# Latent projections between the steps of differential attention, gate chunks between the units of latent attention

## Chip, cores and metric
The kernel runs on one core of a Trainium2 chip. The metric is the device time of one execution in microseconds, the median of several. In the text PE is TensorE, PEld its weight loads, DVE VectorE, ACT ScalarE, POOL GpSimd and SP SyncE.

## What is computed
Two transformer blocks on 512 tokens of width 1024, in float32. Cut to what matters here:

```python
xn = rmsnorm(x, norm_mix_g)
q_lat, kv_lat, k_rope, dq, dk, dv, gate_pre = split(xn @ w_in)      # 384, 256, 32, 512, 512, 512, 2048
q  = rmsnorm(q_lat, g_q) @ w_uq                                     # latent attention: 8 heads of 64 + 32
kv = rmsnorm(kv_lat, g_kv) @ w_ukv
o_mla = causal_attention(q with rope, k with shared rope key, v)
o1, o2 = causal_attention(rope(dq)[0 | 1], rope(dk)[0 | 1], dv)     # differential attention: 4 heads, 2 halves of 64
o_diff = rmsnorm(o1 - lam * o2, g_sub) * (1 - lambda_init)
gates = sigmoid(gate_pre + b_gate)
x = x + (g_mla * (o_mla @ w_a) + g_diff * (o_diff @ w_b)) @ w_out
x = x + swiglu(rmsnorm(x, g_ffn)); x = rmsnorm(x, g_final)          # ffn0
mod = silu(c) @ ada_w + ada_b                                       # 9 vectors of 1024, "ada"
# second block: swiglu (ffn1), a mixer of two attentions with gates, swiglu (ffn2),
# each with its norm scaled and shifted by mod
```

## The kernel before
**Products.** Activations lie as 128 features by 512 tokens. Each float32 operand is split into a high and a low part, so a product is three matmuls: high by high, high by low, low by high (`split_product`). Weights come as 311 chunks of 128x1024 in one fixed order (`STREAM`). SP loads a chunk into one of three `RAW` buffers, ACT makes its high half `HI` (`split_hi`), DVE its low half `LO` (`split_lo`), and TensorE uses it, 24 matmuls of 512 columns in most cases. ACT and DVE work two chunks ahead of TensorE. Each engine has its own program, written in a fixed order; semaphores tie them together. No scheduler moves anything.

**First block, stages in order.** `project_in1` makes the input projections: five latent tiles, the shared rope key and eight tiles of queries and keys, 14 chunks. Between them stand the norm of the input and the two latent norms, each a sum of squares by one-column matmuls (`norm_sums`), a root on ACT, a reciprocal on DVE and a spread by transposes (`norm_spread`). DVE takes each tile out of PSUM, scaled, and rotates it (`rope`). `token_major` makes the values, four chunks. `diff_attention` runs 16 pairs of units, a pair for four causal blocks (128 to 512 keys) of each of four heads. At step s TensorE makes the scores of pair s in four banks, the transposes of pair s-2 and the products with the values of pair s-3; DVE takes the maxima and combines the two halves, ACT makes the exponentials and copies the transposes.

Then come the expansions of the latents, five chunks with 102 matmuls, the latent attention `attention(1)`, 32 units in rounds of four, and `merge(0)`: for each of eight output tiles two gate chunks and a branch chunk. Its first part also turns both attention outputs (`turn`). `out_proj(0)`, a norm, and `ffn(0)` follow. The second block's attentions, `attention(2)` and `attention(3)`, already have gate chunks between their units, eight each, one for every round, taken out of bank 7 by ACT.

**ada.** 72 pieces of 128x1024 go through DVE, each multiplied by a column and added to `ACC`. After each eight TensorE sums them (`ada_sum`) and DVE adds the bias (`ada_take`). POOL loads them in two buffers. Eight pieces lie in `merge(0)`, eight in `out_proj(0)`, 56 in the gate and up projections of `ffn(0)`.

## Time and profile before

| | us |
|---|---|
| median of 3 runs | 2048.89 (2043.05 to 2051.16) |
| the profiled execution | 2047.24 |
| its span, first to last instruction | 2045.2 |
| PE busy | 2001.5 (98%) |
| DVE busy | 1030.8 (50%) |
| ACT busy | 708.8 (35%) |
| mean granted TensorE clock | 0.975 |

The span is what the instructions cover; the 2.0 us around it belong to the start and end of the execution. A matmul's recorded end is modelled, and matmuls overlap, so a busy PE isn't one at its peak: the granted clock stands beside it (1.00 is 2.4 GHz, 0.50 is 1.2 GHz). An engine's idle time is put down to what released it.

### The profile page before, as it was taken

The page shows a single profiled execution, that of the slowest core. Times are in us where ns is not written, and L with a number is a line of the kernel's source. Part 1 is how long each engine was busy: PE and PEld are TensorE (multiplying, and loading weights), DVE is VectorE, ACT ScalarE, POOL GpSimd, SP SyncE. Part 2 cuts the span into 40 slices and gives each one's busy share as a digit, 9 for nine tenths or more (in the row PEclk, how much of TensorE's full clock was granted, in tenths as well). Part 3 has the DMA queues.
Part 4 walks back from the last instruction along what each step waited for, and adds up shares of the span by engine and source line. Part 5 has one row for each costly group of instructions (what it writes and reads, how often), then busy time and mean ns, then how long its engine had stood idle before and what let it go on. Part 6 is the DMA issues. An engine that isn't in the chain of part 4 may idle for free. (4 is left out here: it accounts for less than half of the span.)

```text
span 2045.2 us, 25500 instructions
## 1 busy us (share of the span) xinstructions
PE 2001.5 (98%) x9134; PEld 1604.0 (78%) x9142; DVE 1030.8 (50%) x1587; ACT 708.8 (35%) x1196; POOL 78.0 (4%) x113
## 2 busy tenths in 40 slices
PE   8989999999999999999999999999999999999999
PEld 6765778887888888788888877767777878888887
DVE  6664555567656533453334335857833654333322
ACT  5223662234222222332222324435544533223221
POOL 0010000001111100000000010400000000000000
PEclk9885999999999999999999999999999999999999
DMA  5210113455776633233233332221111223232332
GB/s 191 62 62 0 52 32 115 133 164 177 222 220 204 205 102 103 77 105 101 92 99 96 104 102 83 63 62 42 42 42 42 83 82 103 92 103 92 103 103 92
DMA packets 57514, 207.11 MB, mean 101 GB/s; under 512 B 6448, under 2 KB 6576, under 8 KB 57440
## 3 DMA queue, kind: packets, MB, share of 16 engines
q1 hardware_dynamic: 46800, 167.68, 25.9%
q0 software_dynamic: 10640, 38.44, 6.1%
q8 instruction: 47, 0.77, 0.2%
q14 instruction: 27, 0.22, 0.0%
HBM read 203.96 MB, written 2.10 MB: 101 GB/s over the span
## 5 line engine op out<-in xcount | busy, mean ns | idle before, releaser
L1340 DVE TENSOR_TENSOR LO<-RAW,HI 128x1024 fp32r<-128x1024 f32 x311 | 381.8, 1228 | 512.7 <-ACT HI L955 511.1
L389 PE MATMUL PS<-XH,HI 128*128 128x512 f32 x1552 | 625.2, 403 | 8.0 <-DVE LO L1340 4.9
L391 PE MATMUL PS<-XH,LO 128*128 128x512 f32 x1552 | 608.3, 392 | 0.0
L390 PE MATMUL PS<-XL,HI 128*128 128x512 f32 x1552 | 607.6, 392 | 0.0
L955 ACT ACTIVATE HI<-RAW 128x1024 fp32r<-128x1024 f32 x311 | 327.9, 1056 | 586.1 <-PE PS L391 568.3
L389 PEld LDWEIGHTS PS<-XH,HI 128*128 128x128 f32 x1552 | 294.2, 190 | 82.5 <-issue 13.9
L391 PEld LDWEIGHTS PS<-XH,LO 128*128 128x128 f32 x1552 | 293.2, 189 | 62.9
L390 PEld LDWEIGHTS PS<-XL,HI 128*128 128x128 f32 x1552 | 294.2, 190 | 55.0
L389 PE MATMUL PS<-HIDH,HI 128*128 128x512 f32 x528 | 205.4, 389 | 0.0
L390 PE MATMUL PS<-HIDL,HI 128*128 128x512 f32 x528 | 205.4, 389 | 0.0
L391 PE MATMUL PS<-HIDH,LO 128*128 128x512 f32 x528 | 205.4, 389 | 0.0
L390 PEld LDWEIGHTS PS<-HIDL,HI 128*128 128x128 f32 x528 | 99.1, 188 | 20.7
L389 PEld LDWEIGHTS PS<-HIDH,HI 128*128 128x128 f32 x528 | 99.1, 188 | 20.6
L391 PEld LDWEIGHTS PS<-HIDH,LO 128*128 128x128 f32 x528 | 99.1, 188 | 20.4
L1237 ACT ACTIVATE T<-PS 128x512 f32<-128x512 f32 x45 | 26.9, 598 | 164.0 <-PE PS L391 163.8
L1490 DVE SCALAR_TENSOR_TENSOR ACC<-ADA,SM,ACC 128x1024 f32<-128x1024 f32 x57 | 73.0, 1281 | 13.1 <-DMA ADA<-ada 12.9
L1894 DVE TENSOR_TENSOR Y<-T,PS 128x512 f32<-128x512 f32 x45 | 30.9, 688 | 94.2 <-PE PS L391 94.2
L1165 ACT ACTIVATE PT<-PS 128x128 f32<-128x128 f32 (+1 forms) x96 | 42.1, 439 | 84.5 <-PE PS L736 84.4
L1737 DVE TENSOR_REDUCE SM<-PS 128x1 f32<-128x128 f32 (+1 forms) x96 | 47.0, 489 | 32.9 <-PE PS L723 12.9
L1175 ACT ACTIVATE P<-PS,SM 128x128 f32<-128x128 f32 (+1 forms) x96 | 50.5, 526 | 26.7 <-DVE SM L1737 25.6
L326 POOL DMA_DIRECT2D ADA<-ada x70 | 36.9, 528 | 547.5 <-DVE ACC L1488 271.4
L1243 ACT ACTIVATE HIDH<-Y 128x512 f32 (+1 forms) x66 | 41.7, 631 | 25.8 <-DVE Y L1894 25.8
(328 smaller groups left out, 2131.4 us busy)
## 6 DMA issues: line engine op xcount, KB each, us to landing
RAW<-weights SPq DMA_DIRECT2D x311, 512.0 KB, 3.5
ADA<-ada POOLq DMA_DIRECT2D x72, 512.0 KB, 4.6
X<-x_in SPq DMA_DIRECT2D x4, 512.0 KB, 7.0
y_out<-X SPq DMA_DIRECT2D x8, 256.0 KB, 4.6
SQC<-squares SPq DMA_DIRECT2D x1, 320.0 KB, 9.3
T<-positions POOLq DMA_DIRECT2D x1, 256.0 KB, 5.2
POS<-positions POOLq DMA_DIRECT2D x1, 256.0 KB, 3.3
LAMS<-lambdas POOLq DMA_DIRECT2D x1, 128.0 KB, 6.2
```

The source lines that it names most:

```text
L326: pool.dma_start(ADA[j][:], ada[2 * i + (j + 2)]).then_inc(sem(f"ada{j}"), 16)
L389: mm(bank, a, moving[0][:, t, :], start=start, stop=False)
L390: mm(bank, a, moving[1][:, t, :], start=False, stop=False)
L391: ins = mm(bank, z, moving[0][:, t, :], start=False, stop=stop)
L955: A(HI[n0 % 3][:], RAW[n0 % 3][:], ACT.Copy).then_inc(sem("hi_ready"), 1)
L1165: A(at_["PT"][v % 2][:, 0:n], PS[:, 3 + v % 2, 0:n], ACT.Copy).then_inc(sem("pt_copied"), 1)
L1175: A(at_["P"][u % 3][:, 0:n], PS[:, u % 3, 0:n], ACT.Exp, bias=NMX[:, u % 4:u % 4 + 1], accum_out=RSU[:, u % 4:u % 4 + 1]).then_inc(sem("pr ...
L1243: A(HIDH[:, bass.ds(t, 1), :], Y[:, 0:1, :], ACT.Copy).then_inc(sem("hid_hi"), 1)
L1340: V.tensor_tensor(LO[n0 % 3][:], RAW[n0 % 3][:], HI[n0 % 3][:].bitcast(F32), ALU.subtract)\
L1490: V.scalar_tensor_tensor(out=ACC[:], in0=ADA[j][:], scalar=CND[:, kt:kt + 1], in1=ACC[:], op0=ALU.mult, op1=ALU.add).then_inc(sem("ada_add ...
L1737: V.tensor_reduce(NMX[:, u % 4:u % 4 + 1], PS[:, u % 3, 0:n], AX, ALU.max, negate=True)\
L1894: V.tensor_tensor(Y[:, 0, :], SILU[j % 3], PS[:, 2 * (j % 3) + 1, :], ALU.mult)\
```

## The change
The stream's order is new. Eight chunks of queries and keys come first, in pairs of one head, then two value chunks. The differential attention starts when its first head is rotated; the two other value chunks follow its first two scores. From step 2 on, 22 pieces of latent work (`latent_work`) stand between its matmuls, one or two a step (`piece_step`): the six latent input chunks in halves, their norms, and the expansions. They use banks 5 and 6 in turn and bank 7 for the norms, so the scores have three banks, the transposes one and the products one. ACT now takes query, key and latent tiles out unscaled; the input norm's factor is multiplied into the rotary table and the latent roots.

The 16 gate chunks of the first block stand between the units of `attention(1)`, one for two units, in bank 7, taken out by DVE into tiles of their own. After it come the turns, as after `attention(3)`, and `branch(0)`, the same code as the second block's, with the sigmoids. `merge` is gone.

The ada pieces move: 56 stay in the gate and up projections, now the first seven groups, and eight each lie in the first two and the last two output tiles of `ffn(0)`. Its eighth sum stands in the output projection, its ninth in the norm after it, in the place of a matmul that only kept TensorE busy. POOL loads the first two pieces when the latent scores are done. The weights are the same, in another order; no product is added or left out.

```diff
-STREAM = (("in1", 14), ("dv1", 4), ("uq", 3), ("uk", 1), ("uv", 1), ("merge1", 24), ("out1", 8),
+STREAM = (("qk1", 8), ("dv1", 4), ("lat1", 6), ("uq", 3), ("uk", 1), ("uv", 1), ("gates1", 2 * DT),
+  ("branch1", 8), ("out1", 8),
...
+LATENT = ("q0", "q1", "q2", "k0", "k1", "kr", "uq0", "uq1", "uq2", "uq3", "uq4", "uq5", "uk0", "uk1", "uk2",
+          "uk3", "uv0", "uv1", "uv2", "uv3")
...
+def piece_step(p):
+    return 2 + p if p < 5 else 7 + (p - 5) // 2 if p < 15 else p - 3
+LATENT_CHUNKS = {piece_step(2 * c): c for c in range(11)}
...
-    for j in range(2):
-        pool.dma_start(ADA[j][:], ada[j]).then_inc(sem(f"ada{j}"), 16)
...
+    pool.wait_ge(sem("scores"), 2 * NU)
+    for j in range(2):
+        pool.dma_start(ADA[j][:], ada[j]).then_inc(sem(f"ada{j}"), 16)
...
+    def project_qk1():
+        n0 = FIRST["qk1"]
+        behind(0, n0, (0, 1))
+        pe.wait_ge(sem("squares_loaded"), 16)
+        norm_sums(0)
+        for j in range(2, 8):
+            w = chunk(n0 + j, 0, 0)
+            if j >= 4:
+                pe.wait_ge(sem("qk_copied"), j - 3)
+            used(split_product(PS[:, j % 4, :], w, range(8), range(8), (XH, XL)))
             if j == 2:
                 norm_spread(0)
-        released["in_copied"] += len(IN1)
...
+        def sums(k):
+            nt = NORMS[k][0]
+            pe.wait_ge(sem("squared"), NTB[k + 1])
+            if k == 2:
+                pe.wait_ge(sem("normed"), NDB[2])
+            for t in range(nt):
+                for b in range(NB):
+                    ins = mm(S_LAT[:, b:b + 1], LSQ[k][:, t, b * P:(b + 1) * P], SQV["ones"][:, 0:1],
+                             start=t == 0 and b == 0, stop=t == nt - 1 and b == NB - 1)
+            ins.then_inc(sem("sq_summed"), 1)
+        def spread(k):
+            pe.wait_ge(sem("expanded"), k + 1)
+            for b in range(NB):
+                tok = slice(b * P, (b + 1) * P)
+                ins = nc.tensor.transpose(PS[:, 7, tok], RB[:, 1, tok], SQV["ident"])
+            ins.then_inc(sem("rstd"), 1)
+        pe.wait_ge(sem("v_copied"), NB)
+        for k, t in enumerate(("q0", "q1", "q2", "k0", "k1", "kr")):
+            to = bank_for(t)
+            w = chunk(FIRST["lat1"] + k, 0, 0)
+            split_product(to, w, range(4), range(4), (XH, XL), last=False)
+            if t == "k0":
+                sums(1)
+            if t == "k1":
+                spread(1)
+            yield
+            used(split_product(to, w, range(4, 8), range(4, 8), (XH, XL), first=False))
+            yield
+        for j in range(3):
+            w = chunk(FIRST["uq"] + j, 0, 0)
...
+                ins = split_product(to, w, range(3 * r, 3 * r + 3), range(3), (LQH, LQL))
+                if r:
+                    used(ins)
+                else:
+                    ins.then_inc(sem("uq_half"), 1)
+                if r == 0 and j < 2:
+                    (sums, spread)[j](2)
+                yield
+        w = chunk(FIRST["uk"], 0, 0)
...
+        latent = latent_work()
         for s in range(NPAIR + 3):
+            pieces = [p for p in range(22) if piece_step(p) == s]
             if s < NPAIR:
                 p, i = divmod(s, NB)
                 n = P * (i + 1)
-                if s >= 2:
...
+                    pe.wait_ge(sem("qk_rotated"), 2 * p + 2)
                 for r in range(2):
-                    bank = PS[:, SCORE_BANKS[s % 2][r], :]
+                    if 2 * s + r >= 3:
+                        pe.wait_ge(sem("probs"), 2 * s + r - 2)
+                    bank = PS[:, (2 * s + r) % 3, :]
                     mm(bank[:, 0:n], q_diff(2 * p + r, i), k_diff(2 * p + r, n), start=True, stop=False)
                     mm(bank[:, n - P:n], IDENT_B[:], CAUSAL_B[:], start=False, stop=True)\
                         .then_inc(sem("scores"), 1)
+            if s < 2:
+                diff_values(2 + s)
+            if pieces:
+                next(latent)
             if 2 <= s < NPAIR + 2:
                 w = s - 2
+                pe.wait_ge(sem("combined"), w + 1)
                 if w == 0:
                     pe.wait_ge(sem("v_copied"), NB)
-                pe.wait_ge(sem("combined"), w + 1)
-                if w >= 2:
-                    pe.wait_ge(sem("pt_copied"), w - 1)
+                else:
+                    pe.wait_ge(sem("pt_copied"), w)
                 for kb in range(w % NB + 1):
-                    ins = nc.tensor.transpose(PS[:, 3 + w % 2, kb * P:(kb + 1) * P],
+                    ins = nc.tensor.transpose(PS[:, 3, kb * P:(kb + 1) * P],
                                               P1[w % 3][:, kb * P:(kb + 1) * P], SQV["ident"])
                 ins.then_inc(sem("pt"), 1)
+            if len(pieces) == 2:
...
-                if w >= 2:
-                    pe.wait_ge(sem("onorm"), w - 1)
+                if w:
+                    pe.wait_ge(sem("onorm"), w)
                 for kb in range(i + 1):
-                    ins = mm(PS[:, 5 + w % 2, 0:P], PT1[w % 2][:, kb * P:(kb + 1) * P],
+                    ins = mm(PS[:, 4, 0:P], PT0[w % 2][:, kb * P:(kb + 1) * P],
                              DV[:, kb, p * P:(p + 1) * P], start=kb == 0, stop=kb == i)
                 ins.then_inc(sem("pv"), 1)
     def attention(a):
         at_ = ATT[a]
-        n0 = FIRST["gates2"] + DT * (a - 2)
+        n0, per, before = GATE_CHUNKS[a]
...
                 return
-            if u % 4 == 0:
+            if per == 2:
+                blocks = (((), (0, 1, 2)), ((3, 4), (5, 6, 7)))[u % 2][part]
+            elif u % 4 == 0:
...
+                if before + c:
+                    pe.wait_ge(sem("gate_copied"), before + c)
+            ins = split_product(PS[:, 7, :], (n0 + c) % 3, blocks, blocks, (XH, XL),
+                                first=blocks[0] == 0, last=blocks[-1] == 7)
+            if blocks[-1] == 7:
                 used(ins)
         for u in range(NU + 3):
...
                 if a == 1 and u == 2:
                     pe.wait_ge(sem("v_copied"), 2 * NB)
+                    pe.wait_ge(sem("onorm"), AFTER[1])
...
+    def after_attention(a):
+        turn(a - 1, (3,))
+        for f in range(4):
+            pe.wait_ge(sem("onorm"), AFTER[a] + 2 * NB * (f + 1))
+            turn(a, (f,))
...
-            latents(j)
+            if 1 <= j <= 8:
+                act.wait_ge(sem("chunk_used"), n0 + j)
+                dst, scale = QK1[j - 1]
+                A(dst, PS[:, (j - 1) % 4, :], ACT.Copy, scale=scale).then_inc(sem("qk_copied"), 1)
+            if j == 1:
+                table(0, TAB_A1)
+            if j == 9:
+                act.wait_ge(sem("lams_used"), 2)
+                A(LAM[:, 2:4], LAM[:, 0:2], ACT.Exp).then_inc(sem("lam_exp"), 1)
...
+    def latent_copies(p):
+        def done(t):
+            return sem(LATENT_FREE[t][0])
+        if p < 10 and p % 2:
+            k = p // 2
+            act.wait_ge(sem("chunk_used"), FIRST["lat1"] + k + 1)
+            n, t = (1, k) if k < 3 else (2, k - 3)
...
+            if pieces:
+                latent_copies(pieces[0])
+            if s == 2:
+                table(1, TAB_P1)
+            if s in (8, 11):
+                stds(1 if s == 8 else 2)
+            if s in (9, 12):
+                k = 1 if s == 9 else 2
+                for t in range(NORMS[k][0]):
+                    high(k, t)
...
+    def rotate_qk(k):
+        dst = QK1[k][0]
+        v.wait_ge(sem("qk_copied"), k + 1)
+        rope(dst, TAB_A1, "rot_a")
+        V.tensor_tensor(dst, T[:, 0, :], T[:, 1, :], ALU.add).then_inc(sem("qk_rotated"), 1)
+        v.wait_ge(sem("qk_rotated"), k + 1)
...
+                v.wait_ge(sem("pos_loaded"), 16)
+                link(V.tensor_copy(pos, pos.bitcast(I32)))
+                angles(0, pos, "freq_a")
+            if j == 2:
                 lambdas()
...
+                v.wait_ge(sem("table"), 1)
+                for c in range(2):
+                    link(V.tensor_tensor(TAB_A1[:, c, :], TAB_A1[:, c, :], R0[:], ALU.mult))
+            if j >= 3:
+                rotate_qk(j - 3)
...
+            if s == 0:
+                rotate_qk(7)
+            if s == 1:
+                angles(1, TAB_P1[:, 0, :], "freq_p")
+            if s in (8, 11):
+                roots_of(1 if s == 8 else 2)
+            if s in (9, 12):
+                latent_norm(1 if s == 9 else 2)
+            if s == 10:
+                shared_keys()
+            if s == 13:
+                rotate_shared_keys()
+            if s in (14, 15):
+                rotate_queries(s - 14)
...
+            if a == 1 and u % 2 == 0 and 2 <= u <= NU:
+                c = u // 2 - 1
+                v.wait_ge(sem("chunk_used"), n0 + c + 1)
+                V.tensor_tensor(gate_tile(a, c), PS[:, 7, :], R0[:], ALU.mult).then_inc(sem("gate_copied"), 1)
...
-                    ada_piece(16 + 3 * j, 8, i)
+                    ada_piece(0 + 3 * j, 8, i)
...
-                    ada_piece(17 + 3 * j, 8, i)
+                    ada_piece(1 + 3 * j, 8, i)
...
-                    ada_piece(18 + 3 * j, 8, i)
+                    ada_piece(2 + 3 * j, 8, i)
...
                 for g in range(3):
                     split_lo(n0 + 3 * j + g, 6, i)
+                    if f == 0 and isinstance(i, int) and g < 2:
+                        for r in range(2):
+                            ada_piece((64 if i else 56) + 4 * j + 2 * g + r)
                 v.wait_ge(sem("chunk_used"), 6 * i + (n0 + 3 * j + 3))
```

**Order, first place: TensorE in a step of the differential attention.** One step before, with 128 keys. DK and DQ are keys and queries (one tile DQK after), SQC the identity, P the probabilities, PT the copied transposes.

```order
L657 MATMUL PS<-DK,DQ 128x128 [waits probs]
L658 MATMUL PS<-CAUSAL_B,IDENT_B 128x128
L657 MATMUL PS<-DK,DQ 128x128
...
L669 MATMUL PS<-SQC,P_0_86 128x128 [waits pt_copied,combined]
L669 MATMUL PS<-SQC,P_0_86 128x128 x2
L679 MATMUL PS<-DV,PT_1_90 128x128 [waits onorm,pt_copied]
```

The step of the same head's first block after (step 8). LO and HI are weights, XH and XL the input; RB holds a latent norm's reciprocals.

```order
L767 MATMUL PS<-DQK 128x128 [waits probs,qk_rotated]
L768 MATMUL PS<-CAUSAL_B,IDENT_B 128x128
L767 MATMUL PS<-DQK 128x128 [waits probs]
...
L422 MATMUL PS<-XH,HI_55 128x512
...
L783 MATMUL PS<-SQC,P_0_85 128x128 [waits pt_copied,combined]
...
L422 MATMUL PS<-XH,HI_56 128x512 [waits lo_ready,even_free]
...
L694 MATMUL PS<-SQC,RB 128x128 [waits expanded]
...
L795 MATMUL PS<-DV,PT_1_91 128x128 [waits onorm,pt_copied]
```

Twelve matmuls stand ahead of the transposes and twelve behind them, and the transposes of RB, the latent norm's spread, stand ahead of the products with the values.

**Second place: ACT at the start.** Before, three chunks' high halves are made ahead of the first rotary table (TAB_A).

```order
L988 ACTIVATE SM_74<-PS,SM 128x4 [waits sq_summed]
L955 ACTIVATE HI_55<-RAW_52 128x1024 [waits chunk_used,raw0]
L955 ACTIVATE HI_56<-RAW_53 128x1024 [waits chunk_used,raw1]
L955 ACTIVATE HI_57<-RAW_54 128x1024 [waits chunk_used,raw2]
L1014 ACT_TABLE_LOAD
L1014 ACTIVATE TAB_A_84<-Y 128x512 [waits angle]
L1015 ACTIVATE Y<-Y 128x512
L1017 ACTIVATE TAB_A_84<-Y,SM 128x512 [waits absolute]
L969 ACTIVATE SQ<-LATQ 128x512 [waits sq_summed,in_copied] x2
```

After:

```order
L1055 ACTIVATE SM_74<-PS,SM 128x4 [waits sq_summed]
L1019 ACTIVATE HI_55<-RAW_52 128x1024 [waits chunk_used,raw0]
L1095 ACTIVATE DQK<-PS 128x512 [waits chunk_used]
L1081 ACT_TABLE_LOAD
L1081 ACTIVATE TAB_A_83<-Y 128x512 [waits angle]
L1082 ACTIVATE Y<-Y 128x512
L1084 ACTIVATE TAB_A_83<-Y,SM 128x512 [waits absolute]
L1019 ACTIVATE HI_56<-RAW_53 128x1024 [waits chunk_used,raw1]
```

The table stands ahead of the second of them, for chunk 4, and waits for DVE's angles (Y).

**Third place: DVE in the latent attention.** Two units before (OM is the output).

```order
L1737 TENSOR_REDUCE SM<-PS 128x1 [waits probs,scores]
L1756 RECIPROCAL SM<-SM 128x1 [waits probs]
L1760 TENSOR_SCALAR OM<-PS,SM 128x64 [waits pv,dve_link]
L1737 TENSOR_REDUCE SM<-PS 128x1 [waits probs,scores]
L1756 RECIPROCAL SM<-SM 128x1 [waits probs]
L1760 TENSOR_SCALAR OM<-PS,SM 128x64 [waits pv,dve_link]
```

After:

```order
L1881 RECIPROCAL SM<-SM 128x1 [waits probs]
L1885 TENSOR_SCALAR OM<-PS,SM 128x64 [waits pv,dve_link]
L1855 TENSOR_REDUCE SM<-PS 128x1 [waits probs,scores]
L1881 RECIPROCAL SM<-SM 128x1 [waits probs]
L1885 TENSOR_SCALAR OM<-PS,SM 128x64 [waits pv,dve_link]
L1847 TENSOR_TENSOR GATE_1D<-PS,R_75 128x512 [waits chunk_used]
L1855 TENSOR_REDUCE SM<-PS 128x1 [waits probs,scores]
L1419 TENSOR_TENSOR LO_58<-RAW_52,HI_55 128x1024 [waits hi_ready]
```

A gate's scaled copy (GATE_1D) and a split (LO) came in for every two units; the copy stands behind the output scaling that waits for `pv`.

## Rows read from the trace of the kernel before
**Rows 1.** The page: TensorE's granted clock in 40 slices; a chunk's two splits.
```profile
PEclk9885999999999999999999999999999999999999
...
L1340 DVE TENSOR_TENSOR LO<-RAW,HI 128x1024 fp32r<-128x1024 f32 x311 | 381.8, 1228 | 512.7 <-ACT HI L955 511.1
...
L955 ACT ACTIVATE HI<-RAW 128x1024 fp32r<-128x1024 f32 x311 | 327.9, 1056 | 586.1 <-PE PS L391 568.3
```
**Rows 2.** Busy time by stage: us, PE, PEld, DVE, ACT, POOL, clock, DMA.
```profile
12.24:139.13 126.89, 114.32 (x493) 93.14 (x493) 84.70 (x133) 39.93 (x53) 9.12 (x12) 0.93 0.31 98
139.13:209.31 70.18, 68.38 (x218) 39.43 (x217) 34.02 (x95) 26.77 (x85) 0.00 (x0) 0.59 0.01 2
143.50:197.00 53.50, 53.50 (x151) 29.98 (x151) 24.95 (x70) 17.09 (x59) 0.00 (x0) 0.50 0.00 0
209.31:235.09 25.78, 23.41 (x105) 19.07 (x104) 14.84 (x23) 16.27 (x26) 0.00 (x0) 1.00 0.26 82
235.09:284.05 48.96, 48.65 (x336) 38.31 (x337) 27.01 (x96) 36.59 (x130) 0.00 (x0) 0.97 0.04 12
284.05:423.20 139.15, 136.10 (x610) 113.15 (x610) 76.81 (x102) 45.42 (x58) 3.69 (x7) 0.99 0.38 114
1480.60:1576.90 96.30, 96.28 (x485) 69.87 (x492) 33.07 (x94) 39.90 (x108) 0.00 (x0) 1.00 0.14 44
```
**Rows 3.** Timeline of TensorE, differential attention: start, us, line, operation.
```profile
164.44 2.07 PE L657 MATMUL PS<-DK,DQ 64*128 64x512 f32 x2
...
183.51 2.07 PE L657 MATMUL PS<-DK,DQ 64*128 64x512 f32 x2
...
201.79 1.12 PE L657 MATMUL PS<-DK,DQ 64*128 64x512 f32 x2
```
**Rows 4.** TensorE's waits, whole run: us in total, times, longest.
```profile
PE PS L389 <- DVE LO L1340: 4.9, 2, 3.3
PE PS L490 <- DVE DK L1526: 4.6, 1, 4.6
PE PS L463 <- DVE Y L1429: 3.5, 1, 3.5
...
PE PS L718 <- DVE QM L1996: 2.4, 1, 2.4
...
PE PS L389 <- ACT GATE_F L1149: 2.2, 7, 0.7
```
**Rows 5.** Timeline of TensorE at three other places.
```profile
67.24 1.05 PE L440 MATMUL PS<-SQC,RB 128*128 128x1 f32 x8 [1.18 <-DVE RB L1375]
...
118.17 0.63 PE L491 MATMUL PS<-LO,XH 128*128 128x512 f32 x1
...
261.73 1.08 PE L718 MATMUL PS<-KM,QM 96*128 96x512 f32 x2
...
267.56 1.08 PE L718 MATMUL PS<-KM,QM 96*128 96x512 f32 x2
```
**Rows 6.** Timeline of DVE, then of ACT, at the first table of angles.
```profile
36.57 0.43 DVE L1469 TENSOR_SCALAR Y<-Y 128x512 f32<-128x512 f32 x1
36.91 1.22 DVE L1340 TENSOR_TENSOR LO<-RAW,HI 128x1024 fp32r<-128x1024 f32 x1
...
37.03 0.63 ACT L1014 ACTIVATE TAB_A<-Y 128x512 f32<-128x512 f32 x1 [3.88 <-DVE Y L1469]
...
38.21 0.72 ACT L1017 ACTIVATE TAB_A<-Y,SM 128x512 f32<-128x512 f32 x1
```
**Rows 7.** Groups of DVE, then ACT, 20 to 283 us: busy, mean ns.
```profile
L1996 DVE TENSOR_TENSOR QM<-T 32x512 f32<-32x512 f32 x8 | 5.5, 684 | 0.2
...
L1138 ACT ACTIVATION_READ_ACCUMULATOR P<-PS,SM 128x1 f32 x16 | 3.3, 206 | 0.0
...
L1138 ACT ACTIVATE P<-PS,SM 128x512 f32<-128x512 f32 x4 | 2.7, 683 | 0.0
L988 ACT ACT_TABLE_LOAD x2 | 2.6, 1283 | 0.0
```

764 lines of the change are left out of this document (345 added, 419 removed).

## The prediction
> **What bounds the kernel now.** Read three views in this order. First the page: TensorE is busy nearly everywhere, so only two things can give time back, waits of TensorE and stretches of lower clock. The clock row shows the latter: 8, 8 and 5 in the second to fourth of its 40 slices, 9 nearly everywhere else [rows 1]. Then the stages [rows 2]. The differential attention (139.13 to 209.31) takes 70.2 us at a mean clock of 0.59; its middle, 143.5 to 197, is busy without a gap for all 53.5 us at 0.50, while its DVE is busy for 24.95 us and its ACT for 17.09. No engine feeds it too slowly: it is TensorE at 1.2 GHz that sets the time. The timeline shows the price [rows 3]: a score of 512 keys takes 2.07 us at 183.51 and 1.12 at 201.79, once 2.4 GHz is granted again, and a round of four steps takes 183.51 - 164.44 = 19.07 us. Third the waits of TensorE [rows 4]: the projections before this stage lose 4.9 (one of it 3.3 at the start), 4.6 and 3.5 us to DVE, and the stage after it 2.4. All other stages are filled: the latent attention holds 48.65 busy us of 48.96, the merge 136.10 of 139.15 [rows 2].
>
> **The early part, up to the first score of the latent attention.** Before, it runs from 12.24 to 235.09 us, 222.9 us. No matrix work is dropped, so I add up what TensorE has to do at full clock. A chunk of 24 matmuls costs 5.46 us: the merge has 24 of them in 139.15 us less some 8 for its turns. So one matmul of 512 columns costs 0.2275 us.
> - Eight chunks for queries and keys and four for values: 12 x 5.46 = 65.5 us.
> - The differential attention at full clock: four rounds of 19.07 / 2 = 38.1 us.
> - The latent work moved between its steps: six input chunks (144 matmuls) and 102 for the expansions, 246 x 0.2275 = 56.0 us.
> - The norms' sums, 28 blocks at 1.05 / 4 us [rows 5], are 7.4, their three spreads some 1 us.
> - Each change between the two kinds of work costs a little. Attention (3) of the kernel before is built this way: 96.3 us for eight rounds with a gate chunk each [rows 2]. A bare round is 267.56 - 261.73 = 5.83 us [rows 5], so 96.3 - 8 x (5.83 + 5.46) = 6.0 us, over 56 pieces at most 0.11 each; 22 pieces cost 2.4.
>
> That is 170.4 us. It holds only at 2.4 GHz. For that speaks the same attention (3): scores of 64 rows, as here, turns and values of the same kind, with dense matmuls between, and its clock is 1.00 [rows 2]. Now the new waits; five edits put something into a queue ahead of something else.
> - At the start ACT now makes the rotary table ahead of the high half of chunk 4 (the second order piece). Before, DVE's angles ended at 37.0 and the low half followed at once, to 38.13 [rows 6]; TensorE had waited for it for 4.9 - 3.3 = 1.6 us [rows 4]. Now sine, absolute and sine come first, 37.03 to 38.93, then 1.05 for the high half and 1.23 for the low [rows 1, 6]: the low half ends at 41.3, and TensorE waits some 4.8 us. The lambdas and two scalings of the table (3 us) then stand ahead of the next split; it still ends by 45.5, while chunk 4 lasts to 46.7, and from there a rotation and a split (4.2) fit into a chunk.
> - At steps 8 and 11 TensorE reaches a norm's spread one piece (2.7 and 2.0 us) after the transpose. In that time ACT must copy the transpose, make two exponentials (at 512 keys 0.68 + 0.21 us each [rows 7]), copy and square or copy twice a latent tile (1.2 to 1.3), load a table (1.28 [rows 7]) and take the root, and DVE must expand it (1, with the handovers 1.5). That is about 6.0 and 6.5 us, so waits of 3.3 and 4.4. The nearest rows are the 3.5 and 4.6 us that the same norms cost before [rows 4]; from below the bound is 0.
> - The second table, at step 2, puts two table loads and 2 us of ACT ahead of the exponentials of step 3: 1.6 us.
> - Steps 12 to 15 give DVE 4 x 2.2 us of its own (24.95 us of 53.5, by a step of 19.07 / 4 [rows 2, 3]), two splits (2.5), the second latent norm (2.9), one rotation (2.9) and two query rotations of seven operations (4.8 each [rows 7]): 26.7 us. TensorE has 22 us until it needs the result, a wait of 5. From below 0, from above 12 if ACT and DVE wait for one another.
> - Where TensorE has waited the clock falls: after the 4.6 us wait the matmuls at 118.17 still take 0.63 us instead of 0.40 [rows 5], a stretch of some 3.3 us that costs half of itself. Three such dips are 5 us.
>
> Together 170.4 + 4.8 + 7.7 + 1.6 + 5 + 5 = 194.5 us, a gain of 28.4. The 2.4 us wait for the rotated queries goes: DVE has them at step 15. The shared keys on POOL are copied behind step 13, some 25 us before their use.
>
> One rule weighs against this gain. TensorE is busy for all of 143.5 to 197 and stays at 0.50 [rows 2]. The Trainium skill, "TensorE: Matmul & The Clock Gate", section "Part 1: The HAM clock gate", says that idleness throttles the array and that sustained work releases it. By that rule the stage should have come back by itself, and its low clock would belong to no kind of work that one could mend by mixing; the trace disagrees, being busy is not enough here. The third rival is the time that it would give.
>
> **Latent attention with gate chunks, then the branches.** Before, 48.96 + 139.15 = 188.1 us [rows 2]. The gates leave the merge and stand between the units, two chunks a round. TensorE was full in both stages, so this saves no matrix time: 8 x 5.83 = 46.6, 16 x 5.46 = 87.4, 48 pieces at 0.11 = 5.3, 32 turns 4.2, eight branch chunks 43.7. The one bank for gates adds a wait: a new chunk starts when DVE has scaled the last one out, and that copy stands behind the output scaling that itself waits for TensorE (the third order piece). The nearest row is the wait for the same copy on ACT: 2.2 us in 7 waits, the longest 0.7 [rows 4]. I take 0.5 for each of 16, 8 us; between 0 and 11. Sum 195.2, a loss of 7.1 us. It eats the 3 us that the merge spent waiting for its turned outputs and the 2 to 3 us of low clock at the start of the stage.
>
> **ada pieces.** All 72 multiplications and 9 sums stay. The 16 of merge and output projection, each a pass over 128x1024 like a split's 1.23 us [rows 1], were under TensorE's work; now they lie in the first two and last two output tiles of ffn0, some 5 us of DVE a tile beside 66 matmuls, 15 us. POOL starts the loads when the latent scores end, over 50 us before ffn0. If the cover failed, each late split would cost up to 1.3 us. The last sum fills an idle place in the norm; the last modulation, some 1 us on DVE, comes ahead of ffn1's next split. Nothing in all, within 1.5 us either way.
>
> **Sum.** 28.4 - 7.1 = 21.3 us less. The profiled execution took 2047.24 us, 2.0 over its span; by the sum the new one takes 2025.9. The median of the runs, 2048.89, lies 1.65 above the profiled one, and I keep that distance: 2027.6, rounded to 2028 us.
>
> **Rivals.**
> - **The waits are hidden.** ACT and DVE catch up, TensorE never waits at spreads, tail or gates: 7.7 + 5 + 8 + 3.3 (two dips) = 24 us more, 2004 us. For it: both are half idle in these stages. Against: the waits of the same norms before.
> - **DVE becomes the bound.** It has some 79 us to do from step 0 on (35.7 its own, 13.5 for 11 splits, 7.3 norms, 15.4 rotations, 4.1 angles, 3 the rest) in about 130, in a fixed order. If each new wait in the list is twice as long, 7.7 + 1.6 + 5 + 8 = 22 us are lost, 2050 us.
> - **The low clock belongs to no work.** A stretch as long as 143.5 to 197 runs at half clock whatever fills it, so half of its 53.5 us, 26.7, is lost again: 2055 us. For it: nothing in DVE or ACT marks the point where the clock fell. Against: no other dense stage shows it. It is what the rule of the Trainium skill above comes to.
> - **The mixture stays at 1.2 GHz.** This ends slower. From step 2 to 18 TensorE has some 100 us of work at full clock. At 0.50 it takes 200, and the 21 us of waits and dips vanish under it: 79 us lost, 2107 us. It is slower than before from the point where over 21 of those 100 us run at half clock. For it: the transposes and scores that fell to 0.50 are all still there, and steps 2 to 6 and 12 to 15 hold only one piece each. Against: attention (3) at 1.00, with as little between its steps.
>
> **Chances.** Forecast 0.65, own range 2016 to 2040; hidden waits 0.12; DVE 0.11; clock of no work 0.04; half clock 0.08. Out of the 80% range I leave the half clock and the ends: 2004 to 2052. A measurement of this kernel tells some 0.5%, 10 us, from no change. Below 2038.6 lie nearly all of the forecast and the hidden waits, 0.76; within 10 us the DVE and clock rivals and the forecast's edge, 0.15; above, 0.09.
>
> **What would show it.** In the profile of after: clock near 1 from the first differential score to the last; first score of the latent attention at 206 to 208 us; a wait of over 4 us for the low half of chunk 4; two waits at the latent spreads; some 0.5 us for each gate copy; output projection starting at 402. A clock of 0.5 in the fused stage, or DVE busy over nine tenths there, would prove me wrong.

## The result and the profile after

| | before | after |
|---|---|---|
| median, 8 runs each in the same comparison | 2049.32 (2043.05 to 2060.35) | 2061.62 (2052.72 to 2066.81) |
| ratio to before | | 1.0068, 95% interval 1.0036 to 1.0100 |
| the profiled execution, its span | 2047.24, 2045.2 | 2064.44, 2062.4 |
| mean granted TensorE clock | 0.975 | 0.98 |

The change makes the kernel 0.7% slower. The forecast was 2028 us, 21 less than before, so it is wrong in sign and by 34 us in size. A second measurement of the same kernel (after_again below) gave 1.0077 (1.0049 to 1.0106).

First the page of after: its clock row, and the group of the ada pieces on DVE.

```profile
PEclk8988999999999999999999999999999999999999
...
L1576 DVE SCALAR_TENSOR_TENSOR ACC<-ADA,SM,ACC 128x1024 f32<-128x1024 f32 x63 | 80.8, 1282 | 31.4 <-DMA ADA<-ada 31.1
```

The 5 of [rows 1] is gone, yet 8s stand in the third and fourth slice, and in the first, where before had a 9. Then the stages of after as windows (us, busy time and instructions of PE, PEld, DVE, ACT and POOL, granted clock, DMA share, GB/s): from the first matmul to the first differential score, on to the first latent score, on to the output projection, on to the first down matmul of ffn0, on to the first score of `attention(2)`.

```profile
12.35:80.98 68.63, 62.90 (x261) 50.91 (x261) 46.22 (x77) 26.46 (x37) 1.27 (x2) 0.91 0.34 103
80.98:240.41 159.43, 134.24 (x559) 96.95 (x559) 76.55 (x162) 69.50 (x146) 5.61 (x8) 0.87 0.15 44
240.41:433.19 192.78, 186.13 (x947) 149.70 (x946) 90.47 (x190) 82.59 (x187) 1.06 (x2) 1.00 0.22 69
433.19:739.02 305.83, 304.60 (x1389) 250.78 (x1388) 179.44 (x195) 89.92 (x115) 29.68 (x56) 0.99 0.59 186
739.02:1399.16 660.14, 646.85 (x2906) 522.84 (x2904) 317.15 (x410) 210.98 (x286) 39.19 (x41) 0.99 0.32 101
```

Two windows of before to set beside them, the same early part and the stage from the first down matmul on:

```profile
12.24:235.09 222.85, 206.11 (x810) 151.63 (x811) 133.55 (x251) 82.97 (x164) 9.12 (x12) 0.83 0.21 66
729.47:1382.62 653.15, 643.19 (x2876) 519.15 (x2874) 298.48 (x392) 210.97 (x286) 31.72 (x27) 0.99 0.29 91
```

| stage | before | after | forecast |
|---|---|---|---|
| to the first latent score | 222.9 | 228.1 | 194.5 |
| latent attention to output projection | 188.1 | 192.8 | 195.2 |
| output projection to first down matmul | 306.3 | 305.8 | as before |
| first down matmul to `attention(2)` | 653.2 | 660.1 | as before |
| the rest | 662.6 | 663.2 | as before |

So the miss lies in two stages: 33.6 us in the early part, 7 in the one that got the ada pieces. Neither of the prediction's own signs of being wrong appears: the clock of the fused stage (the differential attention with the latent work between its steps, the second window) is 0.87 and not 0.5, and its DVE is busy for 76.55 of 159.43 us, under half. But the first latent score comes at 240.4 us instead of 206 to 208.

**The early part, taken apart.** Busy time times clock is what TensorE had to do at 2.4 GHz, busy time less that is what the low clock cost, and the rest of the window is waiting. For after: 62.90 x 0.91 + 134.24 x 0.87 = 174.0 us of work; 197.1 - 174.0 = 23.1 lost to the clock; 228.1 - 197.1 = 30.9 of waits. The clock has two digits, so each part is good to some 2.5 us.

| early part | length | work | waits | low clock |
|---|---|---|---|---|
| before | 222.9 | 171.1 | 16.7 | 35.0 |
| forecast | 194.5 | 170.4 | 19.1 | 5.0 |
| after | 228.1 | 174.0 | 30.9 | 23.1 |

The work was forecast within 4 us. Against the forecast the waits are 12 us longer, and the low clock costs 18 more. Where TensorE waits, from 12 to 241 us (total, times, longest; the first wait for LO, 4.5 us, ends at the first matmul and is outside the table above):

```profile
PE PS L694 <- DVE RB L1482: 9.8, 2, 5.9
PE PS L422 <- DVE LO L1419: 8.5, 2, 4.5
PE PS L422 <- ACT KM L1204: 3.8, 1, 3.8
PE PS L767 <- ACT P L1244: 2.9, 2, 1.8
PE PS L795 <- DVE OD L1793: 2.2, 3, 1.7
PE PS L686 <- ACT LSQ L1179: 2.1, 1, 2.1
PE PS L526 <- issue: 1.7, 1, 1.7
PE PS L422 <- ACT DV L1227: 1.5, 1, 1.5
```

The timeline of TensorE shows what stands behind such waits: a score at step 4, the first latent sums, both latent spreads, the third piece of the key expansion.

```profile
109.54 0.49 PE L767 MATMUL PS<-DQK 64*128 64x128 f32 x2 [1.76 <-ACT P L1244]
...
136.98 4.54 PE L686 MATMUL PS<-SQC,LSQ 128*128 128x1 f32 x24 [2.12 <-ACT LSQ L1179]
...
155.81 1.11 PE L694 MATMUL PS<-SQC,RB 128*128 128x128 f32 x4 [3.94 <-DVE RB L1482]
...
192.96 1.11 PE L694 MATMUL PS<-SQC,RB 128*128 128x128 f32 x4 [5.89 <-DVE RB L1482]
...
224.39 0.80 PE L422 MATMUL PS<-LKH,HI 128*128 128x512 f32 x1 [3.82 <-ACT KM L1204]
```

The 24 one-column matmuls at 136.98 take 0.19 us each, where eight took 1.05 us before, 0.13 each [rows 5], and the 512-column matmuls run at 0.63 us until 147.8; those behind the first spread until 164.7. Seven such stretches lie in the early part: 12.4 to 18.4, 43.5 to 49, 110.5 to 114, 137 to 147.8, 155.8 to 164.7, 193 to 199.3 and 224.4 to 230. Each starts at a wait of TensorE or within 1 us behind it, the first one at the wait for the first weights. The forecast had three, of 3.3 us each. Not every wait has one: nothing follows the 1.74 us at 69.9 or the 1.51 at 98.4.

### The profile page after: what moved, and what is told of

It is laid out like the page before. It is cut to its first block and busy times, and to the rows that moved or that the text cites. A ratio compares the mean times of both kernels' runs of the same rounds, so it can differ in the third digit from the quotient of the medians.

```text
span 2062.4 us, 25412 instructions
## 1 busy us (share of the span) xinstructions
PE 1996.8 (97%) x9148; PEld 1599.4 (78%) x9148; DVE 1016.0 (49%) x1576; ACT 721.8 (35%) x1215; POOL 77.0 (4%) x113
## 5 line engine op out<-in xcount | busy, mean ns | idle before, releaser
L422 PE MATMUL PS<-XH,HI 128*128 128x512 f32 x1552 | 632.9, 408 | 18.7 <-DVE LO L1419 8.5
L1576 DVE SCALAR_TENSOR_TENSOR ACC<-ADA,SM,ACC 128x1024 f32<-128x1024 f32 x63 | 80.8, 1282 | 31.4 <-DMA ADA<-ada 31.1
```

Of the source, the lines that this page charges most:

```text
L422: mm(bank, a, moving[0][:, t, :], start=start, stop=False)
L1576: V.scalar_tensor_tensor(out=ACC[:], in0=ADA[j][:], scalar=CND[:, kt:kt + 1], in1=ACC[:], op0=ALU.mult, op1=ALU.add).then_inc(sem("ada_add ...
```

## Experiments

The theory after this reading: the mixture does bring the full clock, as forecast, but its queues are too tight, and most waits of some length are paid twice, once itself and once by a stretch at half clock behind it. The main rival: the low clock belongs to the mixture's own short matmuls and would be there without the waits.

Medians are of 9 or 10 runs where nothing else is said. The runs of before beside them had a median of 2046.5 (beside the later spreads, first table and ada sum, and six idle matmuls), 2045.2 (query rotations, splits, second table, stall probe), 2044.4 (one and two idle matmuls, fixed_four, fixed_seven) and 2044.6 (the last three). A ratio given here differs from the quotient of the two medians by up to 0.002.

The single edits are small against the scatter of the runs (some 4 us), so each is read by its stage in the trace too: "early part" is the time from the first matmul to the first latent score, 228.1 us in after. How much a stage scatters by itself can be read where an edit lies elsewhere: the fused stage took 159.4, 159.2, 159.3 and 159.4 us in after, after_again, sum_later and ada_back, so 2 us tell something there; the first stage, the same code in eight traces, took 65 to 69 us, because the stretches at half clock at its start and behind the wait at 43.5 differ in length.

### Later spreads
```diff
-                    if t == "k1":
-                        spread(1)
                     yield
                     used(split_product(to, w, range(4, 8), ...))
+                    if t == "k1":
+                        spread(1)
                     yield
...
-                        if r == 0 and j < 2:
+                        if (j, r) in ((0, 0), (1, 1)):
                             (sums, spread)[j](2)
```


> The changed kernel with both latent spreads (transposes of RB) one piece later: the first behind the second half of the last latent key chunk in step 9, the second behind the second half of the second query chunk in step 12. Nothing else differs. The changed kernel's trace has waits of 3.9 and 5.9 us there, each followed by TensorE at half clock (155.8 to 164.7 and 193 to 198.5). Theory 'each wait brings its own dip': both waits go and the two dips with them, 9.8 + 4.4 + 2.7 = 17 us less, 2061.6 to 2045. Rival 'the low clock there comes from the mixture (one-column sums, transposes, 64-row scores)': only the waits go, 10 us, 2052, and the stretch behind the first spread stays at 0.50. Rival 'DVE and ACT are late anyway': the wait reappears at the first expansion of the queries, under 5 us gained, 2057 or more.

Measured: 2047.90 us, ratio to before 1.0004 (0.9980 to 1.0029). Windows up to the first differential and the first latent score:

```profile
12.29:79.42 67.13, 61.40 (x260) 49.73 (x260) 46.23 (x77) 26.47 (x37) 1.27 (x2) 0.92 0.35 106
79.42:224.90 145.48, 128.55 (x559) 93.58 (x559) 76.24 (x162) 69.59 (x146) 5.61 (x8) 0.92 0.16 48
```

The fused stage is 13.9 us shorter (159.4 to 145.5). By the same arithmetic the early part holds 174.8 us of work, 22.7 of waits and 15.2 of low clock: 8.2 of waits and 7.9 of clock went, the matmuls being the same. (The two waits of 9.8 us are gone; 0.9 and 1.1 us came up elsewhere.) The rival said that only the waits would go, and that the stretch behind the first spread would stay; it is gone. What the edit did not touch stayed: the wait of 2.1 us ahead of the sums and its half clock.

### Later first table
```diff
-                    if j == 1:
+                    if j == 2:
                         table(0, TAB_A1)
```


> The changed kernel with the first rotary table on ACT behind the high half of chunk 4 instead of ahead of it. Theory 'that place alone makes the wait at 39 us': the wait for the low half falls from 4.0 us to some 0.5, and the half clock behind it (43.5 to 48.8) goes: 3.5 + 2.6 = 6 us less, 2055.5. Rival 'the wait only moves': the rotations of queries and keys start 1 to 2 us later and TensorE waits the same at the first scores of step 0 or at the next split, under 2 us gained, 2060.

Measured: 2057.32 us, 1.0070 (1.0040 to 1.0100). The first matmul of chunk 4:

```profile
39.23 0.50 PE L422 MATMUL PS<-XH,HI 128*128 128x512 f32 x1 [0.99 <-DVE LO L1419]
```

The wait falls from 4.0 us to 1.0 and its half clock is gone. The first stage takes 61.8 us instead of 68.6, of which some 1 to 1.5 is the start; the fused stage then takes 2.1 us more, with a half clock at 91.5 that after doesn't have. Net 4 to 5 us in the trace, about as much as the first stage scatters by itself; the median alone could not show it. What is sure is the wait: it is 4.0 us in every trace with the table in its first place.

### Later query rotations
```diff
-                    if s in (14, 15):
-                        rotate_queries(s - 14)
+                    if s in (15, 16):
+                        rotate_queries(s - 15)
```


> The changed kernel with the two query rotations on DVE (seven operations each, 5.8 and 4.9 us in its trace) one step later, behind steps 15 and 16 instead of 14 and 15. Theory 'they stand ahead of the maxima of step 15, behind which the key copies on ACT are late': the wait of 3.8 us for a key copy (KM) with its half clock (223.5 to 230.5) and the 1.7 us for the output scaling go, 3.8 + 3 + 1.7 = 8.5 us less, 2053. Rival 'DVE is full there': the output scalings of steps 16 and 17 wait for the rotations instead, and the products with the values behind them, 3 us gained or less, 2059.

Measured: 2053.81 us, 1.0062 (1.0038 to 1.0086). The piece that waited 3.82 us at half clock:

```profile
217.25 0.50 PE L422 MATMUL PS<-LKH,HI 128*128 128x512 f32 x1 [2.67 <-ACT KM L1204]
```

The fused stage takes 153.6 us instead of 159.4, 5.8 less. The 1.7 us for the output scaling went, but of the 3.8 only 1.1: the four key copies on ACT (0.6 us each) are a limit by themselves. The half clock behind that wait is gone all the same. That was partly luck: the same wait of 2.67 us, in the same place, is followed by half clock in splits_behind (221.6) and in fixed_seven (188.6).

### Splits behind the exponentials
```diff
 # ACT; DVE likewise, behind the combination of its step
-                    if s in LATENT_CHUNKS:
-                        split_hi(FIRST["lat1"] + LATENT_CHUNKS[s])
...
                     if pieces:
                         latent_copies(pieces[0])
+                    if s in LATENT_CHUNKS:
+                        split_hi(FIRST["lat1"] + LATENT_CHUNKS[s])
```
In after the chain to the first spread reads so on ACT, in the timeline:

```profile
148.88 1.06 ACT L1019 ACTIVATE HI<-RAW 128x1024 fp32r<-128x1024 f32 x1 [11.47 <-PE PS L424]
...
151.50 0.37 ACT L1244 ACTIVATE P<-PS,SM 128x128 f32<-128x128 f32 x1 [1.18 <-DVE SM L1809]
...
153.30 1.28 ACT L1055 ACT_TABLE_LOAD   x1
```

And beside it on DVE:

```profile
149.97 1.23 DVE L1419 TENSOR_TENSOR LO<-RAW,HI 128x1024 fp32r<-128x1024 f32 x1 [7.36 <-ACT HI L1019]
151.12 0.48 DVE L1809 TENSOR_REDUCE SM<-PS 128x1 f32<-128x128 f32 x2
```

> The changed kernel with the latent chunks' splits (HI on ACT, LO on DVE) behind the exponentials, latent copies and the combination of their step instead of ahead of the maxima. They are needed two steps later. Theory 'the waits at sums and spreads are longer than forecast because a split of 1.1 and 1.2 us, itself released only by TensorE's last matmul on that buffer, stands ahead of the maxima': TensorE's wait ahead of the first latent sums (2.1 us) goes to 0.5 or less, the spreads' 3.9 and 5.9 shrink by about 2.3 each, and where a wait falls under some 2 us its half clock goes too: 6.5 us of waits and 4 of clock, 10 less, 2051. Rival 'the chain hangs on TensorE's own transposes and exponentials': the waits shrink by under 1 us in all, 2060.

Measured: 2060.65 us, 1.0072 (1.0044 to 1.0100). TensorE's waits:

```profile
PE PS L694 <- DVE RB L1482: 7.2, 2, 4.3
PE PS L795 <- DVE OD L1793: 6.5, 2, 4.0
```

The wait for the squares (2.1) is gone and the spreads' waits fall from 9.8 to 7.2, so the split does stand in that chain. But waits of 2.5 and 4.0 us for the output scaling come up instead of 1.7, with their half clock, and the fused stage takes 161.6 us. The attribution holds, the remedy doesn't: the split is only late for someone else.

This run also says something on the main rival. The latent sums no longer wait, and TensorE has had no wait since 107 us:

```profile
132.15 2.73 PE L686 MATMUL PS<-SQC,LSQ 128*128 128x1 f32 x24
...
137.83 0.63 PE L422 MATMUL PS<-XH,HI 128*128 128x512 f32 x1
```

The sums themselves run at full clock, 0.11 us each, but a few short matmuls later, from about 136.1 to 139.2, the clock is at half. So of the 10.8 us that follow the sums in after, some 3 come without any wait, with the one-column and short matmuls alone; the other 8 or so aren't there in this run, in which the wait is gone. Here the rival is right in part.

### Later second table
```diff
-                    if s == 1:
+                    if s == 5:
                         angles(1, TAB_P1[:, 0, :], "freq_p")
...
-                    if s == 2:
+                    if s == 7:
                         table(1, TAB_P1)
```


> The changed kernel with the second rotary table's angles on DVE at step 5 instead of 1 and the table on ACT at step 7 instead of 2. Theory 'two table loads and three passes on ACT hold the exponentials of step 3': the wait of 1.8 us for a probability at 109.5 and the half clock behind it (110.5 to 114.5, 1.7 us) go: 3.5 us less, 2058, if step 7 with two pieces of matrix work hides the same 4.5 us of ACT. Rival 'the table costs the same wherever it stands': the wait and a longer half clock appear at the transposes of step 8 or the first spread, no gain or up to 4 us lost, 2062 to 2066.

Measured: 2057.62 us, 1.0061 (1.0039 to 1.0084). Step 4's first score and the first spread:

```profile
108.62 0.48 PE L767 MATMUL PS<-DQK 64*128 64x128 f32 x2 [0.34 <-ACT P L1244]
...
154.64 1.11 PE L694 MATMUL PS<-SQC,RB 128*128 128x128 f32 x4 [5.21 <-DVE RB L1482]
```

Theory and rival both came true in part: 1.8 us fell to 0.3 with no half clock behind it, and 3.9 grew to 5.2. The fused stage took 157.0 us, 2.4 less.

### A later sum of the ada pieces
```diff
                 two(0)
                 if f == 0:
+                    two(1)
                     ada_sum(7)
-                with pe.Fori(1, 4) as i:
+                with pe.Fori(2 if f == 0 else 1, 4) as i:
```
The wait in after:

```profile
772.01 2.97 PE L650 MATMUL PS<-SQC,ACC 128*128 128x1 f32 x16 [2.91 <-DVE ACC L1576]
```

> The changed kernel with the eighth sum of the ada pieces on TensorE two output tiles later in the down projection of ffn0 (behind the fourth tile instead of the second). The pieces, their loads and DVE's order are the same. Theory 'the loads of the pieces are too slow for the sum's place': the wait of 2.9 us and the half clock behind it (772 to 779.3) go, some 6.5 us less, 2055, and the stage from the first down matmul to the second block's attention returns from 660.2 to some 654. Rival 'the loads contend with the weight loads or DVE is late with its splits': the stage stays at 660 and the time at 2061.

Measured: 2060.06 us, 1.0080 (1.0051 to 1.0108). The wait is gone and the stage took 654.6 us in this trace, but the time didn't move. The stage was 659.9, 658.5, 661.6, 655.5 and 653.6 in the five kernels above, which all have the sum in its old place, so one trace of it proves little. The two combined kernels below also have the later sum, and there the stage took 656.5 and 660.1 us: the later sum is no sure gain. The undo below had to decide.

### What a wait costs: the stall probe
In the kernel before, out_proj on TensorE and ACT:
```diff
+                    if m in (3, 5, 7):
+                        pe.wait_ge(sem("stall"), 3 * b + m // 2)
...
+                    if m in (3, 5, 7):
+                        for q in range(((1, 5, 10), (3, 8, 15))[b][m // 2 - 1]):
+                            A(SM[:, 85:86], EPSC, ACT.Copy)  # each waits for the last
...
```


> The kernel before, in which TensorE has to wait six times in dense matmul work (ahead of the fourth, sixth and eighth chunk of both output projections, some 11 us apart) for a chain of 2, 6, 11 and 4, 9, 16 small copies on ACT. It measures what a wait costs besides itself. Theory 'the clock falls by the length of the wait': waits under some 2 us leave the matmuls behind them at full speed, longer ones put a stretch of 3 to 6 us behind them at half clock (0.63 instead of 0.40 us each), so that a wait of 4 us costs 6 or more. Rival 'the half clock in the changed kernel's fused stage comes from its one-column and short matmuls': no wait here is followed by more than 3.3 us at half clock, whatever its length.

One run, 2066.22 us. The six waits (the edit makes each of them wait for the chain on ACT; what stands in the brackets is inferred by the profile):

```profile
431.46 0.47 PE L389 MATMUL PS<-MH,HI 128*128 128x512 f32 x1 [1.62 <-ACT SM L1230]
...
445.14 0.47 PE L389 MATMUL PS<-MH,HI 128*128 128x512 f32 x1 [2.52 <-DVE LO L1352]
...
461.59 0.76 PE L389 MATMUL PS<-MH,HI 128*128 128x512 f32 x1 [3.69 <-issue]
...
1651.31 0.47 PE L389 MATMUL PS<-MH,HI 128*128 128x512 f32 x1 [2.09 <-ACT SM L1230]
...
1665.69 0.77 PE L389 MATMUL PS<-MH,HI 128*128 128x512 f32 x1 [3.22 <-DVE LO L1352]
...
1684.50 0.77 PE L389 MATMUL PS<-MH,HI 128*128 128x512 f32 x1 [4.86 <-issue]
```

| wait, us | 1.62 | 2.09 | 2.52 | 3.22 | 3.69 | 4.86 |
|---|---|---|---|---|---|---|
| matmuls at 0.63 us behind it, us | 0 | 0 | 3.3 | 6.0 | 5.2 | 4.3 |
| cost: the wait and half of that stretch | 1.6 | 2.1 | 4.2 | 6.2 | 6.3 | 7.0 |

With nothing but dense 512-column matmuls around them, the four waits of 2.5 us and more were each followed by half clock, for up to 6.0 us, and the two of 1.6 and 2.1 by none. That refutes the rival as expected of this run, that no stretch would be longer than 3.3 us; it doesn't say that short matmuls bring no half clock of their own. Two things don't fit a simple price: the stretch isn't longer for a longer wait, and in the mixture 1.76 us was enough once while 2.12 and 3.94 us were followed by 10.8 and 8.9. The Trainium skill, "TensorE: Matmul & The Clock Gate", section "HAM oscillation — how this bites in real kernels", has an example in which each wait for data brings some 1.67 us of throttled time; here none of these stretches is as short as that.

This run brought a surprise. Its differential attention is the code of before, yet it took 56.2 us instead of 70.2. Two windows in it:

```profile
145.00:166.00 21.00, 21.00 (x61) 11.37 (x59) 10.39 (x29) 7.53 (x27) 0.00 (x0) 0.52 0.00 0
166.00:193.00 27.00, 25.36 (x126) 14.57 (x126) 19.50 (x57) 13.61 (x47) 0.00 (x0) 0.99 0.00 1
```

The same kind of work ran at 0.52 and then at 0.99. In the profile of before it stayed at 0.50 to 197 [rows 2]. And the runs of before, 29 in the first comparison, spread over 20 us in step with their clock: 2033.6 at a mean of 0.982, 2053.7 at 0.972. So the length of that stretch differs from run to run with nothing changed, 21 us in one trace and over 53.5 in the other; that it also makes the spread of the times is argued from the clock, two traces don't show it.

### Idle matmuls in the kernel before
```diff
                             pe.wait_ge(sem("probs"), 2 * s - 2)
+                        for t in range(6):   # 2 in filler_two, 1 in filler_one
+                            mm(PS[:, SCORE_BANKS[s % 2][0], :], XH[:, t, 0:P], XH[:, t, :], ...)
                         for r in range(2):
```


> The kernel before with six more matmuls of 512 columns (the input's high part by itself) ahead of the scores of each of the 16 steps of the differential attention, written into the score bank and overwritten: 96 matmuls, 21.8 us at full clock, that compute nothing. Theory 'this stage runs at half clock for want of dense matmuls between its own': the clock goes to near 1.00 and the stage takes 38.1 + 21.8 = 60 to 64 us instead of 70.2, so the kernel with more work is 6 to 10 us faster than before, 2041. Rival 'the low clock belongs to no kind of work': the stage stays at 0.50 and takes 70.2 + 43.7 = 114 us, 2093.

> The kernel before with two idle matmuls of 512 columns ahead of the scores of each step of the differential attention instead of six (filler_before): 32 in all, 7.3 us at full clock. With six the stage took 65.5 us at clock 1.00, so 65.5 - 21.8 = 43.7 us without them. Theory 'a few dense matmuls a step hold the clock': 43.7 + 7.3 = 51 us instead of 70.2 in the profiled execution, the time 18 us under before, 2028, with a smaller scatter. Rival 'two are not enough': stretches at 0.50 remain, the stage takes 60 us or more, and the runs scatter over some 20 us like those of before (2034 to 2054 here).

> The same with one idle matmul a step, 3.6 us. If the clock holds: 43.7 + 3.6 = 47.3 us for the stage, 22 under before, 2024. If it holds in part only: 55 to 65 us and a wide scatter, 2032 to 2042. In the stall probe, whose code in this stage is that of before, the stage began at 0.50 and returned to 1.00 at 166 with nothing else in it, so the outcome here also tells whether that return was chance.

The differential attention with six idle matmuls a step:

```profile
141.98:207.46 65.48, 63.55 (x307) 39.77 (x307) 33.52 (x95) 25.82 (x84) 0.00 (x0) 1.00 0.00 1
```

With two:

```profile
140.45:192.76 52.31, 50.87 (x247) 29.86 (x247) 33.10 (x95) 26.63 (x85) 0.00 (x0) 0.97 0.00 1
```

With one:

```profile
140.68:190.12 49.44, 48.08 (x233) 28.53 (x232) 33.03 (x95) 26.71 (x85) 0.00 (x0) 0.97 0.00 1
```

| | stage | median | range of the runs | ratio to before |
|---|---|---|---|---|
| before, beside six | 70.2 (profiled before) | 2046.5 | 2033.6 to 2053.7 | |
| before, beside two and one | | 2044.4 | 2032.9 to 2052.2 | |
| six (filler_before) | 65.5 | 2049.81 | 2044.9 to 2051.7 | 1.0023 (1.0006 to 1.0041) |
| two | 52.3 | 2031.92 | 2028.9 to 2037.9 | 0.9946 (0.9927 to 0.9965) |
| one (5 runs) | 49.4 | 2027.91 | 2025.6 to 2030.3 | 0.9922 (0.9894 to 0.9949) |

More matmuls, less time. With six the stage is 4.7 us shorter although it has 21.8 us more to do. Its profiled execution, 2044.95 us, is shorter than that of before, 2047.24, by 2.3 of these 4.7 us; the rest is lost ahead of the stage, which starts 2.8 us later, mostly by a half clock at the very start (12.3 to 16) that the trace of before doesn't have. That the median isn't shorter was not expected. One idle matmul a step, 3.6 us of work that computes nothing, gives 16.5 us of the 21 that the whole change was forecast to give, and its slowest run (2030.3) is faster than the fastest of before (2032.9). So the low clock of this stage did belong to its kind of work, as the forecast's sum had it, and mixing in real work wasn't needed to lift it.

### Four edits together, and seven
fixed_four has the later spreads, ada sum, first table and query rotations. fixed_seven adds the later second table, the first latent sums one piece later (with the squares on DVE that they sum) and another bank order for the values, so that only the last block of tokens waits for the last key tile:
```diff
-        DV_BANKS, FV_BANKS = (5, 6, 3, 4), (0, 1, 2, 5)
+        DV_BANKS, FV_BANKS = (5, 6, 4, 3), (0, 1, 2, 5)
...
-                    if t == "k0":
-                        sums(1)
                     yield
                     used(split_product(to, w, range(4, 8), ...))
+                    if t == "k0":
+                        sums(1)
```


> The changed kernel with four of the single edits together: latent spreads later, eighth ada sum later, first table later, query rotations later. Alone they gave, by stages of their traces, 13.9, 5.5, 4.8 and 5.8 us. Theory 'each wait and the half clock behind it are separate losses': the sum, 30 us, so 2061.6 - 30 = 2031.6, that is under before by some 15. Rival 'the gains overlap, and a wait removed comes back at the next handover': half of it, 2046, level with before.

> fixed_four with three more: the second table at step 7 with its angles at step 5, the first latent sums one piece later (behind the second half of the fourth latent chunk) and the values' bank order turned so that only the last block waits for the last key tile. Waits that these touch in the changed kernel: 1.8 with 4 us of half clock, 2.1 with 10.5 us of half clock, 1.7. Theory as for fixed_four: 3.5 + 7 + 1.7 = 12 less, 2020. Rival 'the later table and sums make the first spread wait again': 5 us back with a half clock of 9 us, 2027.

Measured: fixed_four 2033.99 us, 0.9959 (0.9934 to 0.9984); fixed_seven 2026.06 us in 5 runs, 0.9909 (0.9879 to 0.9939). The early part of fixed_four:

```profile
12.19:213.66 201.47, 184.82 (x818) 139.66 (x819) 121.71 (x239) 95.99 (x183) 6.95 (x10) 0.95 0.23 70
```

The same part of fixed_seven, in its two stages:

```profile
12.38:72.17 59.79, 58.82 (x260) 48.18 (x260) 46.16 (x77) 26.48 (x37) 1.27 (x2) 0.97 0.39 119
72.17:203.56 131.39, 120.82 (x559) 87.97 (x559) 75.22 (x162) 69.30 (x146) 5.68 (x8) 0.97 0.18 53
```

| early part | length | work | waits | low clock |
|---|---|---|---|---|
| after | 228.1 | 174.0 | 30.9 | 23.1 |
| fixed_four | 201.5 | 175.6 | 16.7 | 9.2 |
| fixed_seven | 191.2 | 174.3 | 11.5 | 5.4 |

The work is the same in all three, and so are the matmuls. 19 us of waits went, and 18 of low clock with them. Four edits gave 26.6 us in the early part, a little more than the 13.9 + 4.8 + 5.8 that they gave alone; 3 us of it are the half clock at the start, which no edit touches and which this trace happens not to have. The sums and the second table are fed in time once they stand where the chain can reach them. The 24 sums bring no half clock in fixed_seven, where transposes and a piece of dense matmuls follow them instead of products and scores: the edit moved them out of a row of short matmuls as well as out of a wait, so the two causes aren't told apart there.

### The ada pieces back, and after once more
```diff
 # branch(0) and out_proj(0) on DVE; sums, takes and modulation as before
+                    if b == 0:
+                        ada_piece(m)
...
-                                    ada_piece((64 if i else 56) + 4 * j + 2 * g + r)
```


> The changed kernel itself once more, for a second trace and more times beside the two others. It should take 2059 to 2062 us. If the loss in the down projection of ffn0 is fixed, its stage from the first down matmul to the second block's attention takes 660 us again with a wait of 2 to 3 us at the eighth ada sum; if that wait depends on how the loads fall, it is anywhere from 0 to 3 (in the kernels with the sum in its place it was 2.9, 2.6, 1.6, 1.5 and twice none).

> The changed kernel with the 72 ada pieces, their nine sums and the modulation where the kernel before has them: eight pieces in the branch chunks, eight in the output projection, 56 in the gate and up projections, none in the down projection, and the idle matmul back in the norm. Theory 'the move to the down projection costs 5 to 7 us': that stage returns from 660.1 (658.2 in the mean of six traces) to 653.1, output projection and branches stay within 2 us, and the time falls by 4 to 6, to 2056. Rival 'the pieces were better where they are now, behind the latent attention they delay DVE': the branches or the output projection lose 3 us or more and the time stays at 2060.

> fixed_seven without its later ada sum but with the ada pieces back as in ada_back: all edits found by these runs in one kernel. fixed_seven took 2026.1 with 660.1 us in the stage of the down projection; if the ada move costs 5 to 7 us whatever stands ahead, this one takes 2020 to 2022. If the waits there only depend on chance, it takes 2025 or more.

Measured: after_again 2058.41 us, 1.0077 (1.0049 to 1.0106); ada_back 2055.79 us, 1.0063 (1.0037 to 1.0088); six_ada_back 2021.70 us in 4 runs, 0.9895 (0.9844 to 0.9945). The stage from the first down matmul to `attention(2)` in after_again:

```profile
737.46:1394.45 656.99, 647.03 (x2906) 524.65 (x2904) 317.06 (x410) 210.95 (x286) 39.12 (x41) 0.98 0.32 102
```

In ada_back:

```profile
737.00:1389.06 652.06, 641.57 (x2875) 518.10 (x2874) 298.52 (x392) 211.04 (x286) 31.75 (x27) 0.99 0.30 91
```

In six_ada_back:

```profile
703.80:1356.56 652.76, 641.83 (x2876) 518.08 (x2874) 298.31 (x392) 210.93 (x286) 31.73 (x27) 0.99 0.30 91
```

With the pieces in the down projection the stage takes 653.6 to 661.6 us in seven traces with the sum in its place, 658.0 in the mean; with the pieces back it takes 652.1 and 652.8, and 650.4 to 653.2 in before and the four kernels made from it. The move costs some 5 us there. The wait for the sum is a part of it: the four traces in which TensorE waited for 1.5 us or more took 658.5 to 661.6 us, the three in which it waited for 0.4 us or not at all 653.6 to 657.0. In after_again TensorE waited for the sum for only 0.3 us and the stage was still 4.9 us longer than in ada_back. By a finer sum of busy time times clock, some 2 us of that are work, the 30 more matmuls, and 3 are half clock, 11 us of it at the norm behind the down projection (863 to 874) where ada_back, and after itself, have 7. The sums stood in other stages before, so a part of the price only moved: from the first latent score to the first down matmul the kernels took 1.5 us more with the pieces back (500.1 against 498.6 in after) and, in six_ada_back, 2.5 more (501.6 against 499.1 in fixed_seven). That leaves some 3 to 4 us of loss in all. The medians fit but don't prove it: after_again to ada_back is 2.6 us and fixed_seven to six_ada_back 4.4, and in both pairs the intervals of the ratios overlap. six_ada_back is the fastest version by its median, 1% under before.

## Why the prediction was wrong

**What bounds the kernel now: right.** TensorE at half clock in the differential attention, and waits around it. The fillers show it. What the reading missed is that the length of that half clock differs from run to run. The forecast took the profiled execution's 53.5 us as fixed; by luck the median of before lies near that execution, so this didn't spoil the number.

**The work of the early part: right.** 170.4 us forecast, 174.0 measured, 174.3 in fixed_seven. Mixed with dense matmuls the stage runs at full clock where TensorE doesn't wait, in after everywhere, in the other runs with one clear exception, the 3 us behind the sums in splits_behind.

**The waits: too small, the first half of the miss.** 30.9 us instead of 19.1. The low half of chunk 4 cost 4.0 (forecast 4.8) and the second table 1.8 (1.6). The two spreads were put at 3.3 and 4.4 and took 3.9 and 5.9. One of the two rows beside them was misread: the 4.6 us of [rows 4] are the wait of the first value matmul for a key tile (DK), not for a norm. And the list of what stands ahead of them had no split in it, and splits_behind took away 2.6 by moving the splits. The tail, put at 5 us, came to 7.8 (1.7, 3.8, 1.3, 0.5 and two of 0.2); of its 3.8 us 2.7 hang on four key copies on ACT and not on DVE, as rotations_later shows. The rest was on no list: 1.7 for the last key tile's bank, 1.5 for the value copies, 2.1 for the first latent sums, 0.9 and 1.1 for a latent part and a probability, 7.4 in all. The forecast priced the places that it had picked from the diff; these five weren't among them.

**The clock behind the waits: the step that failed.** "Three such dips are 5 us" rested on one row at 118.17 [rows 5], 1.65 us each. There are seven, and they cost 23.1 us, 3.3 each. Their number was wrong because of the waits above, their size by taking the shortest stretch in sight. The trace of before had a longer one: the wait of 1.18 us at 67.24 that [rows 5] shows is followed by half clock to about 75.1, some 7 us.

```profile
68.16 1.64 PE L444 MATMUL PS<-SQC,SQ 128*128 128x1 f32 x8
...
74.50 0.63 PE L391 MATMUL PS<-XH,LO 128*128 128x512 f32 x1
```

The stall probe shows up to 6.0 us at half clock in dense work, after 10.8 and 8.9 behind the sums and the first spread. The low clock is 18 of the 33.6 us by which the early part missed. About 3 of them are the stretch at the start (12.4 to 18.4), which was on no list; in other traces of the same code it lasts 0 to 7 us, so that part is chance. That the rest is mostly a price of the waits and not of the mixture is shown by spreads_later, in which waits and low clock went together and the work stayed, and borne out by fixed_four and fixed_seven. Not all of it: splits_behind has 3 us behind the sums with no wait.

**Latent attention and branches: right.** A loss of 7.1 forecast, 4.7 measured. The gate waits came to 5.4 us in 14 waits instead of 8 in 16, their sizes as forecast:

```profile
PE PS L422 <- DVE GATE_1M L1847: 3.6, 7, 0.8
PE PS L422 <- DVE GATE_1D L1847: 1.8, 7, 0.3
```

**The ada pieces: wrong.** "Nothing in all, within 1.5 us either way"; it costs about 5 us in the down projection's stage and 3 to 4 in all. The step named the passes on DVE (5 us beside 15) and the early start of the loads, and forgot that there are two buffers: from the third piece on, a load starts when a piece is done and lands 4.6 us after its issue. DVE waits 31.1 us for ada loads in after's page, 17.3 of it in the down projection, and waited 12.9 for them in before:

```profile
L1490 DVE SCALAR_TENSOR_TENSOR ACC<-ADA,SM,ACC 128x1024 f32<-128x1024 f32 x57 | 73.0, 1281 | 13.1 <-DMA ADA<-ada 12.9
```

TensorE stood for the sum up to 2.9 us. That isn't the whole price, since the stage is longer than before's without this wait too; the sums and the half clock at the norm have a part in it, and how the rest divides stays open.

**The rivals.** None of them is what happened. "The low clock belongs to no work" came nearest in time with 2055 us, "DVE becomes the bound" (2050) in kind, by doubled waits, but DVE was busy for only 76.6 of the 159.4 us of the fused stage: what bounded was the order in which ACT and DVE do their things, not their load. "The low clock belongs to no work" is refuted by the idle matmuls, though its observation, that nothing marks the point where the clock falls, was a fair warning. The rule of the Trainium skill named beside it ("TensorE: Matmul & The Clock Gate", "Part 1: The HAM clock gate"), that sustained work releases the clock, is borne out in part: in the stall probe the clock did come back at 166 with nothing changed, in the profile of before it didn't come back until 197. The case that ended slower than before was put on the mixture staying at 1.2 GHz; it ended slower by waits that bring their own half clock, a case that was on no list and should have had most of the chance for "slower".

## What to carry to other kernels

When short matmuls run at half clock for long, first put one idle dense matmul beside them and measure: here 16 of them gave 16.5 us, nearly as much as a rebuilt schedule after seven repairs (18.3). When work is fused into such a stage, give every result that crosses engines one more piece of matrix work than its chain needs, split and table load included, and price a wait that remains with the half clock behind it: in the stall probe 2.5 to 4.9 us of waiting cost 4.2 to 7.0. A work item with two buffers moved into a shorter stage needs its loads counted, not only its passes.

## What the runs showed of the hardware that was not expected

- The same code at the same place ran at half clock for 53.5 us in one execution and for some 21 us in another, with the full clock behind it; in 29 runs the time of before follows its mean clock over 20 us (0.982 at 2034, 0.972 at 2054). One profile of such a stage is one draw. With an idle matmul in each step the runs lay within 5 us.
- In the stall probe waits of 2.5 to 4.9 us were followed by 3.3 to 6.0 us at half clock, in dense work; in after the stretch was up to 10.8 us where one-column matmuls or transposes came first. Its length didn't grow with the wait.
- The half clock can come without a wait: in splits_behind 24 one-column matmuls and a few short ones were followed by 3 us of it, 25 us after the last wait.
- The same wait isn't always followed by it: 1.5 us for the value copies were in table_later (91.5) and not in after (98.4), 2.67 us for the key copies in fixed_seven and not in rotations_later. What decides it stays open, and so does why 1.76 us were enough in after at 109.5 while 2.09 us were not in the stall probe, and why the six idle matmuls shortened the stage but not the median.
